# A mixer's recurrence with its filling work spread over the links, a mixer's tail in another order, and products that nobody reads

## The reference

```python
for layer in range(2):                    # first block
    xn = rms_norm(h, norm_mix_g[layer])
    # layer 0: gated linear attention and RWKV-7; layer 1: RG-LRU and mLSTM
    h = h + concatenate([y_a, y_b]) @ w_mix_out[layer]
    h = h + memory_cross_attention(rms_norm(h, ...), mem_n, wq, wkv, wo)
    h = h + conv_glu_ffn(rms_norm(h, ...), w_up, conv_w, conv_b, w_down)
x = rms_norm(h, final_norm_g)
h = modulate(rms_norm(x, g_pre_mix), shift_m, scale_m)     # second block
y = hybrid_mixer(h, w_in, ...)            # dilated attention beside HGRN-2
x = x + gate_m * rms_norm(y, g_post_mix)
h = modulate(rms_norm(x, g_pre_ffn), shift_f, scale_f)
y = moe_ffn(h, w_router, ..., w_gu, w_down)   # 32 experts, top 4 of each token
x = x + gate_f * rms_norm(y, g_post_ffn)
```

## Time and profile before

| | us |
|---|---|
| three runs | 2410.25, 2404.24, 2409.98 |
| median | 2409.98 |
| the profiled execution, its own time | 2404.27 |
| its span from the first to the last instruction | 2402.5 |
| busy: TensorE's products / weight loads | 2274.5 / 1484.3 |
| busy: VectorE / ScalarE / GpSimd | 673.8 / 381.2 / 135.3 |
| read from memory | 597.29 MB |

### The profile page before, as it was taken

The page is one execution under the profiler, slowest core; times in us unless marked ns, Lnnn a source line. Parts: engine busy times, 40 slices in busy tenths (PEclk is TensorE's granted clock), DMA queues, the critical chain, the costliest instruction groups (busy, mean ns, idle before and its releaser), DMA issues.

```text
span 2402.5 us, 25830 instructions
## 1 busy us (share of the span) xinstructions
PE 2274.5 (95%) x10905; PEld 1484.3 (62%) x10905; DVE 673.8 (28%) x1326; ACT 381.2 (16%) x686; POOL 135.3 (6%) x191
## 2 busy tenths in 40 slices
PE   8999989999999999999999799999999999999995
PEld 5887778888878888888767643333334433333332
DVE  3344422334354132335243321111111111111112
ACT  4321112100024121000231410000000000000001
POOL 0113300000000000000000010000000000000000
PEclk9999989999999999999999899999999999999998
DMA  6211043443542335347432269999999899999994
GB/s 237 105 71 36 1 187 116 148 155 140 223 163 118 140 140 210 132 166 290 174 125 79 99 259 428 428 427 427 427 427 426 357 380 427 428 427 427 427 427 183
DMA packets 43323, 600.08 MB, mean 250 GB/s; under 512 B 5232, under 2 KB 5504, under 8 KB 6688
## 3 DMA queue, kind: packets, MB, share of 16 engines
q1 hardware_dynamic: 43200, 598.36, 61.0%
HBM read 597.29 MB, written 1.05 MB: 249 GB/s over the span
## 4 chain that ended last, share of the span: by engine, by line
PE 84%; DMA 11%; DVE 3%; ACT 1%; issue 0%; SPq 0%; PEldq 0%; DVEq 0%; ACTq 0%
PE pb L402 82%; DMA ring<-in_gu 8%; DMA arena<-in_dne 3%; PE pb L412 2%; DVE arena L304 1%; DVE arena L319 1%; DMA arena<-in_dn 1%; ACT arena L363 0%; ACT xs L363 0%; ACT xt L363 0%; DMA col<-in_cols 0%; DVE ring L319 0%; SPq L533 0%; DVE mix L304 0%; PEldq L2976 0%
## 5 line engine op out<-in xcount | busy, mean ns | idle before, releaser
L402 PE MATMUL pb<-arena 128*64 128x512 f32 (+9 forms) x2332 | 681.6, 452 | 26.0 <-DMA ring<-in_gu 14.3
L402 PE MATMUL pb<-ring,arena 128*64 128x512 f32 x1648 | 481.0, 595 | 0.9 <-DMA ring<-in_dne 0.9
L402 PE MATMUL pb<-xt,ring 128*128 128x256 f32 (+3 forms) x1808 | 402.9, 384 | 8.7 <-ACT xt L363 4.9
L402 PEld LDWEIGHTS pb<-arena 128*64 128x64 f32 (+4 forms) x2332 | 278.2, 163 | 202.2 <-issue 175.9
L402 PEld LDWEIGHTS pb<-xt,ring 128*128 128x128 f32 (+3 forms) x1808 | 339.6, 189 | 67.3 <-issue 12.9
L402 PE MATMUL pb<-kv,arena 128*64 128x512 f32 (+2 forms) x592 | 259.1, 592 | 36.3 <-DMA arena<-in_dne 35.5
L402 PEld LDWEIGHTS pb<-ring,arena 128*64 128x64 f32 x1648 | 153.5, 137 | 198.3 <-issue 198.3
L402 PEld LDWEIGHTS pb<-kv,arena 128*64 128x64 f32 (+1 forms) x592 | 86.9, 151 | 193.8 <-issue 191.3
L369 ACT ACTIVATE arena<-pb 128x512 f32<-128x512 f32 (+2 forms) x131 | 74.4, 568 | 629.2 <-PE pb L412 420.8
L304 DVE TENSOR_TENSOR mix<-pb,mix 128x512 f32<-128x512 f32 x68 | 47.0, 692 | 429.5 <-PE pb L402 429.5
L363 ACT ACTIVATE arena<-arena 128x512 f32<-128x512 f32 (+4 forms) x151 | 86.4, 572 | 298.4 <-DVE arena L319 272.0
(11 more groups left out here) (178 smaller groups left out, 1948.0 us busy)
## 6 DMA issues: line engine op xcount, KB each, us to landing
ring<-in_gu SPq DMA_DIRECT2D x67, 2048.0 KB, 19.0
arena<-in_gu SPq DMA_DIRECT2D x48, 2048.0 KB, 17.2
ring<-in_dne SPq DMA_DIRECT2D x32, 2048.0 KB, 13.4
arena<-in_dne SPq DMA_DIRECT2D x18, 2048.0 KB, 17.6
kv<-in_gu SPq DMA_DIRECT2D x17, 2048.0 KB, 15.8
kv<-in_dne SPq DMA_DIRECT2D x16, 2048.0 KB, 13.0
ring<-in_up SPq DMA_DIRECT2D x13, 2048.0 KB, 7.9
ring<-in_ada SPq DMA_DIRECT2D x9, 2048.0 KB, 7.9
```

What stands on the lines that cost most here:

```text
L402: r = self.e.matmul(out, lhsT, rhs, start=start, stop=stop, skip_group_check=True)
```

## The change

**First mixer.** State 15, which nothing reads, is left out. The rows of the second half are done chunk by chunk: in `link(c)`, behind state c, stand the eight small products of chunk c and one side step. The first half's mean is in link 8 and its variance in link 10. On VectorE the first half's normalization is a generator, of which each link takes one step. The scratch area is given back in link 8. In the output projection the second half's mean stands ahead of block 1 and its variance ahead of block 3.

**Third mixer.** The final norm's sum moves ahead of the first projection, and ScalarE's root with it; the attention passes two side steps instead of four before it turns its output, and VectorE reaches that point ahead of its second gate; the outputs and the head sums of the output projection are taken one at a time (blocks 4, 5, 6, 7); VectorE multiplies by the gate ahead of the head norms instead of between them.

**Router.** ScalarE squares block b before it scales block b - 1. The logits run over the channel blocks outside and the two halves inside. Four groups of products of the identity with a constant of 256 columns, 10, 6, 3 and 5 of them, are written to banks that nobody reads: behind the sum `pa.ss`, behind the gate vector, behind the turned activations, and ahead of the first gather.

```diff
+    def warm(self, name, lhsT, rhs, n):
+        b = self.tile(name)
+        for k in range(n):
+            self.mm(b[:, 0:rhs.shape[-1]], lhsT, rhs, True, True, sig=name if k == n - 1 else None)
+        self.free(name)
...
-        def staggered(chunk_pair, states, rows, end, each=None):
+        def staggered(chunk_pair, states, rows, link, each=None):
...
             for c in range(8, 16):
-                states(c)
-                if c in (9, 11):
-                    end("m" if c == 9 else "v", 0)
-            for j in range(4):
-                rows(1, j)
+                if c < 15:
+                    states(c)
+                link(c)
...
+            def link(c):
+                if c == 8:
+                    end("m", 0)
+                elif c == 10:
+                    end("v", 0)
+                if c == 8:
+                    rows.bank = P.tile("rw.y1", hold=True)
+                    P.wait_ge("free c7.r")
+                elif c == 15:
+                    P.wait_ge("free rw.s14")
+                for j in range(4):
+                    row(1, j, c, None if j < 3 else "rw.y1" if c == 15 else f"rw.y1.{c}")
+                if c == 8:
+                    P.used("rw_scratch")
+                elif c == 15:
+                    P.release("rw.y1")
+                P.advance(1)
...
-            P.used("rw_scratch")
             P.drain("rw.d")
...
-                   before={2: lambda: end("m", 1), 5: lambda: end("v", 1)})
+                   before={1: lambda: end("m", 1), 3: lambda: end("v", 1)})
...
+            first = end(0)
+            staggered(chunk_pair, states, lambda j: add_rows(0) if j == 3 else None, lambda c: next(first, None))
+            add_rows(1)
+            for half in (first, end(1)):
+                for _ in half:
+                    pass
...
             P.m.put("due at.o", P.steps + 1)
-            for _ in range(4):
+            for _ in range(2):
                 yield True
...
             sum_p(P, "m2", MIX)
-            proj_p(P, "in2.0", "at.q", xn="m2", after_first=lambda: sum_p(P, "fin"))
+            sum_p(P, "fin")
+            proj_p(P, "in2.0", "at.q", xn="m2")
...
-                   before={1: lambda: state(4), 2: lambda: state(5), 3: lambda: state(6), 5: outputs, 7: means},
+                   before={1: lambda: state(4), 2: lambda: state(5), 3: lambda: state(6), 4: lambda: outputs(0),
+                           5: lambda: outputs(1), 6: lambda: mean(0), 7: lambda: mean(2)},
                    at_last={3: lambda: squares(0), 5: lambda: squares(1), 7: lambda: squares(2)})
             squares(3)
+            P.warm("pa.w", ident, cst["tri"], 10)
...
             shifted_s(S, 0, "m2")
+            root_s(S, "fin", out=RB1)
...
             state(0)
+            V.reach("hg.s1")
             gate(2)
...
             for j in (0, 2):
+                V.wait_ge(f"hg.sq{j}")
+                V.tt(Fr[:, j:j + 2, :], Fr[:, j:j + 2, :], GR[:, j:j + 2, :], MUL)
+            for j in (0, 2):
                 head_root_v(V, f"hg.h{j}", KN[:, j:j + 2, :], Ke[:, j:j + 2, :], 128)
-                V.tt(Fr[:, j:j + 2, :], Fr[:, j:j + 2, :], GR[:, j:j + 2, :], MUL)
...
+            P.warm("mo.w0", ident, cst["tri"], 6)
...
-            for i in range(2):
-                for c in range(8):
-                    P.wait_ge(f"mo.x{c // 2}")
-                    P.mm(b[:, i * 32:i * 32 + 32], XT[:, c, i * 128:(i + 1) * 128], w[:, c, :], c == 0, c == 7,
-                         sig="mo.lg" if (i == 1 and c == 7) else None)
+            for c in range(8):
+                P.wait_ge(f"mo.x{c // 2}")
+                for i in range(2):
+                    P.mm(b[:, i * 32:i * 32 + 32], XT[:, c, i * 128:(i + 1) * 128], w[:, c, :], c == 0 and i == 0,
+                         c == 7, sig="mo.lg" if (i == 1 and c == 7) else None)
             back_p(P, XT, "mo.t")
+            P.warm("mo.w1", ident, cst["tri"], 3)
...
                 S.mark(f"mo.q{b}")
-                for c in (2 * b, 2 * b + 1):
-                    S.act(XT[:, c, :], HT[:, c, :], ACT.Copy, scale=CB1[:, c:c + 1])
-                S.mark(f"mo.g{b}")
+                if b:
+                    gained(b - 1)
             root_s(S, "mo")
+            gained(3)
...
         def moe_p(P):
+            P.warm("mo.w2", ident, cst["tri"], 5)
             route_p(P, 0, JOBS[0])
```

More of the change, by code:

```diff
@@ L1286, in staggered @@
                 if FIRST_Y <= tick < FIRST_Y + 4:
[L1287 removed]
+                    rows(tick - FIRST_Y)
                 if each is not None:
@@ L1374, in states, with row, rows @@
                              sig=f"rw.s{c}" if (j == 3 and hh == 1) else None)
[L1376 to L1386 removed]
+            def row(i, j, c, sig):
+                for hh in range(2):
+                    pr, o = half64[hh], j * 128 + (c - 8 * i) * 16
+                    P.mm(rows.bank[pr, o:o + 16], U[pr, j, c - 1, :], RP[pr, j, c * 16:(c + 1) * 16], True, True,
+                         sig=sig if hh else None)
+            def rows(j):
+                if j == 0:
+                    rows.bank = P.tile("rw.y0", hold=True)
+                    P.wait_ge("free c3.r", "free rw.s7")
+                for c in range(1, 8):
+                    row(0, j, c, None if c < 7 else "rw.y0" if j == 3 else f"rw.y0.{j}")
+                if j == 3:
+                    P.release("rw.y0")
+            def link(c):
[15 more added lines that the diff above has]
+                P.advance(1)
             def end(what, i):
@@ L1397, in end @@
                     P.mm(b, blk64, K[:, :, h], True, True, sig=f"rw.v{i}")
-            staggered(chunk_pair, states, rows, end, lambda tick: P.advance(1))
-            P.used("rw_scratch")
+            staggered(chunk_pair, states, rows, link, lambda tick: P.advance(1))
             P.drain("rw.d")
@@ L1436, in end, with link @@
                     S.mark(f"rw.e{i}")
-            staggered(chunk_pair, lambda c: None, lambda i, j: None, end)
+            def link(c):
+                if c == 8:
+                    end("m", 0)
+                elif c == 10:
+                    end("v", 0)
+            staggered(chunk_pair, lambda c: None, lambda j: None, link)
+            S.fill("rw.d")
             end("m", 1)
@@ L1521, in rwkv_v, with add_rows, end @@
-            staggered(chunk_pair, states, rows, end)
-            end("m", 1)
-            end("v", 1)
+            def add_rows(i):
+                b = V.tile(f"rw.y{i}").rearrange("p (j t) -> p j t", j=4)
+                o = 16 if i == 0 else 0
+                y = Y0[:, :, i * 128 + o:(i + 1) * 128]
+                V.tt(y, b[:, :, o:128], y, ADD)
+                V.free(f"rw.y{i}")
+            def end(i):
+                h = half_of[i]
+                b = V.tile(f"rw.m{i}").rearrange("p (j t) -> p j t", j=4)
+                V.stt(R[:, :, h], b, -1.0 / 64, Y0[:, :, h], MUL, ADD)
+                V.free(f"rw.m{i}")
+                V.mark(f"rw.q1{i}")
+                yield
+                V.wait_ge("rw.gg")
+                V.tt(KK[:, :, h], R[:, :, h], GG[:, :, h], MUL)
+                yield
+                yield
+                yield
+                b = V.tile(f"rw.v{i}").rearrange("p (j t) -> p j t", j=4)
+                r, t = K[:, :, h], EP[:, :, h]
+                V.wait_ge(f"rw.e{i}")
+                V.stt(t, b, 64 * 64e-5, r, ADD, MUL)
+                V.free(f"rw.v{i}")
+                yield
+                V.stt(t, t, -0.5 / 64, r, MUL, MUL)
+                yield
+                V.stt(r, t, 1.5, r, ADD, MUL)
+                yield
+                V.tt(KK[:, :, h], KK[:, :, h], r, MUL)
+                yield
+                V.tt(MIX[:, 4:8, h], KK[:, :, h], BON[:, :, h], ADD)
+                V.mark(f"rw.mix{i}")
@@ L2660, in moe_head_s, with gained @@
             S.begin("moe")
+            def gained(b):
+                for c in (2 * b, 2 * b + 1):
+                    S.act(XT[:, c, :], HT[:, c, :], ACT.Copy, scale=CB1[:, c:c + 1])
+                S.mark(f"mo.g{b}")
             for b in range(4):
```

74 lines of the change are left out of this document (17 added, 57 removed).

## The result

The changed kernel takes 2369.32 us (median; 2365.98 to 2371.64), the kernel before 2408.96 us (2404.24 to 2410.25) beside it: a ratio of 0.984, interval 0.982 to 0.986. The profiled execution took 2368.39 us with a span of 2366.6 us; before, 2404.27 and 2402.5.

What follows compares the result with a forecast made beforehand. TensorE's start on the first expert was taken to set the end, as the experts' weight stream behind it is rigid. Gains 15.5 + 4.0 + 14.5 + 7.0 = 41 us, from 2407 to 2366 us; range 2356 to 2384.

Steps and rivals of the forecast that it cites:

- What bounds the kernel: The end is the moment TensorE starts the first expert plus a constant; every us gained ahead shortens the whole.
- Part 1: First mixer's end: links of some 2.0 us without idle time, 19.4 us against 34.9; gain 15.5 us.
- Part 2: Third mixer's start: the final norm's sum fills TensorE's 4.89 us wait before the first projection; gain 4.0 us.
- Part 3: Third mixer's tail: gain 11.4 us from reordering plus 3.1 us from a held clock, together 14.5 us.
- The remaining gap: Third mixer's output pass: TensorE still idles 2.0 us between VectorE's first and second operands.
- Part 4: Router's stretch and unread products: logits 4.0, exponential 0.9, gather 2.6, sum 7.5 us; 7.0 taken.
- the 0.9 us for the exponential: Router: transposes end early enough that ScalarE's exponential no longer holds VectorE, idle 1.05 us before; gain 0.9 us.
- 0.5 for handovers: Router: some tenths allowed for handovers before the first expert's product, so 7.0 us taken from a sum of 7.5.
- what is next late: First expert's product needs a bank freed by VectorE's first copy of Y; VectorE's chain moves by only 4.9 us.
- 1.00 from there to the experts: Sign of a right forecast: granted clock 1.00 from the second output pass's gap of about 2 us to the experts.
- Rival 2: Clock falls in the logits and transposes don't bring it back; part 4 is worth 1.6, 2371 us; chance 12%.
- Rivals 1, 3, 4 and 5: 1: clock falls in links, 2381, 8%; 3: part-3 gaps stay, 2374, 5%; 4: rigid end, 2407, 2%; 5: slower, 2421, 1%.

## Why the prediction was right

Predicted: 2366 us, range 2356 to 2384. Measured: 2369.32 and, again, 2371.97. The profiled pair of executions differs by 35.9 us, the medians by 39.6 and, the second time, by 33.8; the sum said 41.

- **What bounds the kernel.** Right: 36.25 us earlier at the first expert product and 35.9 at the end. The stretch of the experts did not care.
- **Part 1**, 15.5 us, measured 14.3, and 14.6 undone alone. A link is 2.10 us and not 2.0, and the end of the chain has some tenths more. The clock in the links, the one cost that no row priced, is 1.00 as chosen, and the run without side steps shows how near the other end was: the same small products alone lost it.
- **Part 2**, 4.0 us, measured 4.2, and 4.1 undone alone.
- **Part 3**, 14.5 us, measured 13.0, and 13.1 undone alone. Mis-sized term: state and column block in turn were taken at 2.53 us a pair and are 3.01 (1.09 us from the start of the state's eight records to the next block, which the sum had at some 0.7). Three pairs give 1.4 of the 1.5 us. The trace of the kernel before had the right price: a block starts at 1300.58 and the next one, behind a state, at 1303.58. The remaining gap is 1.81 us, where I said 2.0, and the clock held.
- **Part 4**, 7.0 us, measured 4.2. This is the step that failed. Up to the end of the logits it went as worked out: 3.7 us against 4.0. Then the clock fell at the end of the logits, the transposes took 3.57 us, and the 0.9 us for the exponential did not come (VectorE waits 0.98 us for it, 1.05 before), while VectorE's new wait of 0.41 us for the ranks came on top; the gather gave 2.5 of its 2.6; and the second fall behind the biases took 1.7 back where I had put 0.5 for handovers. I had named VectorE's first copy of Y as what is next late, and so it is, but it moved by 3.3 us against the head's start (41.2 to 37.9) where I had 4.9. With it the part is worth 5.5 us, which the execution with the old tail had (45.29 - 39.74); the second fall takes the other 1.4. So my sign "1.00 from there to the experts" did not come. My reason for a held clock was that the waits were full. They were, and it fell nevertheless.
- **Rival 2** (12%) was half right: the clock falls in the logits. But the transposes did not hold it down: it is back by some 1342.5 (0.89 at 1342 to 1344), with nothing but transposes since 1339.1. The Trainium skill ("TensorE: Matmul & The Clock Gate", Part 4: PE-mode transpose) says that the fast clock doesn't engage for transposes, which don't count as busy in the same way; here, as in the earlier trace rows, the trace shows a rise at the end of such a stretch. The run with needed work in the waits shows it more plainly. It has 32 transposes in a row from 1343.03; the clock is 0.50 at 1345 to 1346 and 1.00 at 1347 to 1348, and the last sixteen take 1.91 us (lines above), the price of the higher level. It isn't always so: with no unread product the clock stays at 0.50 from 1340 through the transposes (1345.10 to 1348.75) to 1356. The page's sentence is thus contradicted in some executions and not in others, and what lets the clock rise here stays open. Rivals 1, 3, 4 and 5 did not happen: no fall in the links, no 2.5 us gaps, no rigid end, no loss.
- **By luck**: a later start (+1.7 us) and a fall of the clock near 740 us that the kernel before had and the changed one didn't (some 1.7 of the 2.2 us in the table) nearly cancel. Neither is in the change: with the code of the changed kernel up to there, the first state came anywhere from 292.5 to 298.2 us, and the stretch of 809.88 us took up to 811.99.

What stays open is what sets the record at which the clock falls in the head. Equal code lost it once in some executions and twice in others; no run here varied that alone. Nor did I combine the two last ideas, needed work in the waits with the biases spread among wide products: the run with thin ones in a row says only that the row is bad.

## What to carry to other kernels

Before a wait is filled, ask who ends it and what the engine does behind it. If another engine's last result ends the whole group, filling is worth nothing by itself (first group: 0 us), and it pays only where the level that it keeps up reaches work that TensorE itself limits (the other three: some 2 to 3 us). A side stream of full-width work inside a chain of small products can pay by the clock alone (2.7 us here, with 0.7 us idle to hide in). Price a term from a row of its own shape where the trace has one (the pair of 3.0 us in part 3). And read an experiment of one stretch in that stretch: equal code elsewhere moved by up to 5.6 us between executions.

## What the hardware showed that I had not expected

- The granted clock (1.2 or 2.4 GHz) fell with TensorE busy, behind thin products: to 0.50 at the end of 32 records of 32 columns (at 1339, with 0.06 us idle since 1330.5) and again behind 8 records of 32 rows by 512 columns; and behind the bare links, some 240 small records with 0.7 us idle in 11.4. A long idle wait isn't needed. In the links a side step in each kept it at 1.00. For the other two places, that thinness is the cause is argued: only the biases were spread out, in a single run, and with them in a row the clock held in nine of twelve executions.
- A record's price at a level says nothing of whether it keeps that level: in the changed kernel the eight bias records ran at full speed (3.70 us) and the sixteen transposes behind them paid (3.13 instead of 1.97 us).
- A group of products that computes nothing but is wide did better in a wait than needed ones that are thin: a head of 41.1 against 42.2 us, in one profiled execution of the one and two of the other. The times (2371.97 and 2369.0 us) don't show it.
